# Expert weights of a routed layer in twelve transfers per expert instead of six

## The reference

```python
for e in range(N_EXPERTS):
    hh = xf @ w_expert_in[e] + b_expert_in[e]            # (264, 2048)
    gate = min(hh[:, :1024], 7); lin = clip(hh[:, 1024:], -7, 7)
    act = (lin + 1) * gate * sigmoid(1.702 * gate)
    y += comb[:, e:e+1] * (act @ w_expert_out[e] + b_expert_out[e])
```

## Time and profile before

| | us |
|---|---|
| median of 3 runs | 1761.41 (1759.38 to 1762.2) |
| profiled execution, own time | 1761.88 |
| its span, first to last instruction | 1760.1 |
| TensorE busy with products | 1566.7 (89% of the span) |
| VectorE / ScalarE / GpSimd busy | 306.7 / 208.8 / 143.8 |
| read from HBM / written | 507.62 MB / 30.50 MB |
| chain that ended last | 65% TensorE, 28% DMA, 3% VectorE |
| granted TensorE clock, mean | 0.939 of full speed |

### The profile page before, as it was taken

One profiled execution on the slowest core, in us unless ns is written; L12 is line 12 of the kernel. 1 busy time (PEld: TensorE's weight loads), 2 busy tenths in 40 slices (PEclk: granted clock), 3 DMA queues, 4 the chain that ended last, 5 costly groups with the idle time before them and its releaser, 6 DMA issues.

```text
span 1760.1 us, 18050 instructions
## 1 busy us (share of the span) xinstructions
PE 1566.7 (89%) x6938; PEld 755.9 (43%) x6939; DVE 306.7 (17%) x597; ACT 208.8 (12%) x369; POOL 143.8 (8%) x202
## 2 busy tenths in 40 slices
PE   5899999799949688999998999989898999999894
PEld 2687887651138465433333333333333333333331
DVE  1000000424341013211211111111111111111113
ACT  2100000424320001101000000000000000000001
POOL 0040000000107000000000000000000000000000
PEclk9899999889989889899999999999999999999997
DMA  8565656317950345555899999999999999999992
GB/s 316 188 224 188 238 191 229 108 48 282 336 196 28 143 161 221 202 206 235 339 424 418 422 424 418 420 420 422 418 427 419 412 413 414 409 421 419 426 417 81
DMA packets 78729, 533.55 MB, mean 303 GB/s; under 512 B 7290, under 2 KB 8402, under 8 KB 51842
## 3 DMA queue, kind: packets, MB, share of 16 engines
q1 hardware_dynamic: 66896, 502.35, 70.2%
q0 software_dynamic: 9952, 24.61, 4.6%
q10 hardware_dynamic: 1849, 6.16, 1.0%
HBM read 507.62 MB, written 30.50 MB: 306 GB/s over the span
## 4 chain that ended last, share of the span: by engine, by line
PE 65%; DMA 28%; DVE 3%; ACT 2%; SPq 1%; issue 1%; ACTq 0%; DVEq 0%; POOL 0%; POOLq 0%
DMA ring<-in_w_expert_in_dram 23%; PE ps L517 15%; PE ps L790 14%; PE ps L811 14%; PE ps L673 3%; PE ps L445 3%; PE ps L602 2%; PE ps L671 2%; PE ps L707 2%; PE ps L754 1%; PE ps L590 1%; PE ps L762 1%; DMA ring<-in_w_up_ret_dram 1%; PE ps L495 1%; PE ps L581 1%
## 5 line engine op out<-in xcount | busy, mean ns | idle before, releaser
L790 PE MATMUL ps<-ring,xgT 128*64 128x512 f32 x1632 | 409.9, 648 | 40.9 <-DMA ring<-in_w_expert_in_dram 40.9
L517 PE MATMUL ps<-hT,ring 128*128 128x264 f32 x1152 | 261.3, 389 | 4.7 <-ACT hT L896 4.7
L790 PEld LDWEIGHTS ps<-ring,xgT 128*64 128x64 f32 x1632 | 121.7, 148 | 305.5 <-issue 251.2
L811 PE MATMUL ps<-moe_ring,actT 128*64 128x512 f32 x1088 | 242.7, 599 | 0.4 <-ACT actT L1007 0.4
L517 PEld LDWEIGHTS ps<-hT,ring 128*128 128x128 f32 x1152 | 219.9, 192 | 49.5 <-issue 6.7
L811 PEld LDWEIGHTS ps<-moe_ring,actT 128*64 128x64 f32 x1088 | 78.1, 137 | 140.4 <-issue 135.5
L1293 DVE COPY xg<-ps 128x512 f32<-128x512 f32 x35 | 24.2, 691 | 622.8 <-PE ps L754 622.8
L790 PE MATMUL ps<-moe_ring,xgT 128*64 128x512 f32 x544 | 122.5, 592 | 0.0
L754 PE MATMUL ps<-rows,picked 128*64 128x512 f32 (+1 forms) x420 | 101.4, 599 | 1.6 <-ACT x_rows L991 1.6
L1003 ACT ACTIVATE glu_s<-glu_g 128x512 f32<-128x512 f32 x34 | 21.4, 629 | 448.8 <-DVE glu_g L1305 448.8
L790 PEld LDWEIGHTS ps<-moe_ring,xgT 128*64 128x64 f32 x544 | 39.1, 137 | 77.7 <-issue 77.7
(11 more groups left out here) (254 smaller groups left out, 986.3 us busy)
## 6 DMA issues: line engine op xcount, KB each, us to landing
ring<-in_w_expert_in_dram SPq DMA_DIRECT2D x96, 2048.0 KB, 16.5
moe_ring<-in_w_expert_out_dram SPq DMA_DIRECT2D x64, 2048.0 KB, 10.7
moe_ring<-in_w_expert_in_dram SPq DMA_DIRECT2D x32, 2048.0 KB, 18.1
ring<-in_w_in_dram SPq DMA_DIRECT2D x18, 2048.0 KB, 8.0
ring<-in_w_ada_dram SPq DMA_DIRECT2D x12, 2048.0 KB, 11.4
ring<-in_state_ret_dram SPq DMA_DIRECT2D x8, 2048.0 KB, 11.5
out_dram<-ring POOLq DMA_DIRECT2D x8, 2048.0 KB, 11.5
ring<-in_w_up_ret_dram SPq DMA_DIRECT2D x4, 2048.0 KB, 13.9
```

Source lines behind the costliest of these rows:

```text
L517: mm = nc.tensor.matmul(ps[:, j, 0:T], ring[s][:, k, j * P:(j + 1) * P], hT[:, k, :], start=(k == 0), stop=(k == KC - 1))
L790: mm = nc.tensor.matmul(side(bank, g), xgT[:, 2 * j + a, :], w[:, a, c * COL:(c + 1) * COL], start=False, stop=(j == 3 and a == 1))
L811: mm = nc.tensor.matmul(side(2, g), actT[:, 4 * h + a, :], w[:, a, g * COL:(g + 1) * COL], start=False, stop=(h == 1 and a == 3))
```

## The change

- Each of the six chunks becomes two of 1 MB, 8 KB in each partition, in half of the old place: eight (j = 0 to 7) for `w_expert_in`, of 128 rows each, one row in a partition; four (8 to 11) for `w_expert_out`, of 256 rows each, two in a partition. SP issues twelve transfers for an expert, and each is waited for by itself.
- The places in memory stay as they were; two new chunks lie where an old one lay. TensorE's order is the same: what stood after old chunk 0 now stands after new chunks 0 and 1, and so on. The number and size of its products are the same.
- The uses of all eight input chunks count on one semaphore (`in_used`), those of the four output chunks on another (`out_used`), instead of one for each chunk. Both are raised at the start by one item's worth. Every wait on them is rewritten to a count. Most come at the same instruction as before; those of GpSimd on the first chunk of either kind come after the first half of the old chunk.
- The transposes read contiguous columns for the input chunks, and every second for the output chunks.
- Three semaphores that nothing used are gone (`c_sig`, `rstd_ready`, `osq_free`), and so are the six of `chunk_used`.

```diff
-CHUNKS = 6
+SLOTS_IN, SLOTS_OUT = 8, 4
+CHUNKS = SLOTS_IN + SLOTS_OUT
...
-        moe_ring = list(ring) + [new(f"moe_ring{s}", [P, KC, COL]) for s in range(RING, CHUNKS)]
+        for s in range(3):
+            new(f"moe_space{s}", [P, KC, COL])
+        half_at = [ring_at + size([P, KC, COL]) * s for s in range(RING)] + [work + size([P, KC, COL]) * s for s in range(3)]
+        moe_ring = [at(f"moe_ring{j}", [P, 2 * D], half_at[j // 2] + size([P, 2 * D]) * (j % 2)) for j in range(CHUNKS)]
...
             def expert(e, j):
-                if j < 4:
-                    src = w_expert_in[0, e, 2 * P * j:2 * P * (j + 1)].rearrange("(p a) n -> p (a n)", a=2)
+                if j < SLOTS_IN:
+                    src = w_expert_in[0, e, P * j:P * (j + 1)]
                 else:
-                    src = w_expert_out[0, e, COL * (j - 4):COL * (j - 3)].rearrange("(p a) n -> p (a n)", a=4)
-                sp.dma_start(moe_ring[j][:].rearrange("p k n -> p (k n)"), src).then_inc(moe_loaded[j], 16)
+                    src = w_expert_out[0, e, 2 * P * (j - SLOTS_IN):2 * P * (j - SLOTS_IN + 1)].rearrange("(p a) n -> p (a n)", a=2)
+                sp.dma_start(moe_ring[j][:], src).then_inc(moe_loaded[j], 16)
...
-                for j in range(CHUNKS):
-                    sp.wait_ge(chunk_used[j], due)
+                for j in range(SLOTS_IN):
+                    sp.wait_ge(in_used, due * SLOTS_IN + (j + 1))
                     expert(e, j)
+                for h in range(SLOTS_OUT):
+                    sp.wait_ge(out_used, due * SLOTS_OUT + (h + 1))
+                    expert(e, SLOTS_IN + h)
...
+            pe.sem_inc(in_used, SLOTS_IN)
+            pe.sem_inc(out_used, SLOTS_OUT)
...
             def hidden(j, e):
                 pe.wait_ge(moe_loaded[j], e * 16 + 16)
-                w = moe_ring[j][:].rearrange("p k n -> p (k n)").rearrange("p (a n) -> p a n", a=2)
-                for a in range(2):
-                    for bank in range(2):
-                        for g in range(2):
-                            c = 2 * bank + g
-                            mm = nc.tensor.matmul(side(bank, g), xgT[:, 2 * j + a, :], w[:, a, c * COL:(c + 1) * COL],
-                                                  start=False, stop=(j == 3 and a == 1))
-                mm.then_inc(chunk_used[j], 1)
+                for bank in range(2):
+                    for g in range(2):
+                        c = 2 * bank + g
+                        mm = nc.tensor.matmul(side(bank, g), xgT[:, j, :], moe_ring[j][:, c * COL:(c + 1) * COL],
+                                              start=False, stop=(j == SLOTS_IN - 1))
+                mm.then_inc(in_used, 1)
...
-                for h in range(2):
-                    pe.wait_ge(moe_loaded[4 + h], e * 16 + 16)
-                    w = moe_ring[4 + h][:].rearrange("p k n -> p (k n)").rearrange("p (a n) -> p a n", a=4)
-                    for a in range(4):
+                for h in range(SLOTS_OUT):
+                    j = SLOTS_IN + h
+                    pe.wait_ge(moe_loaded[j], e * 16 + 16)
+                    for a in range(2):
                         for g in range(2):
...
-                    mm.then_inc(chunk_used[4 + h], 1)
+                    mm.then_inc(out_used, 1)
...
-                act_e.wait_ge(chunk_used[3], q + 1)
+                act_e.wait_ge(in_used, q * SLOTS_IN + 2 * SLOTS_IN)
...
-                pool.wait_ge(chunk_used[0], q + 1)
+                pool.wait_ge(in_used, q * SLOTS_IN + (SLOTS_IN + 1))
```

More of the change, by code:

```diff
@@ L320, in trunk_kernel @@
         moe_loaded = [sem(f"moe_loaded{s}") for s in range(CHUNKS)]
-        chunk_used = [sem(f"chunk_used{s}") for s in range(CHUNKS)]
+        in_used, out_used = sem("in_used"), sem("out_used")
         picked_ready, slots_ready, slots_taken = sem("picked_ready"), sem("slots_ready"), sem("slots_taken")
@@ L419, in _ @@
                 due = sp.value_load(cum_i[0:1, e - 1:e], min_val=1, max_val=ITEMS)
-                for j in range(CHUNKS):
-                    sp.wait_ge(chunk_used[j], due)
+                for j in range(SLOTS_IN):
+                    sp.wait_ge(in_used, due * SLOTS_IN + (j + 1))
                     expert(e, j)
+                for h in range(SLOTS_OUT):
+                    sp.wait_ge(out_used, due * SLOTS_OUT + (h + 1))
+                    expert(e, SLOTS_IN + h)
             items = sp.value_load(cum_i[0:1, E - 1:E], min_val=E, max_val=ITEMS)
-            for j in range(2):
-                sp.wait_ge(chunk_used[j], items)
+            for j in range(1):
+                sp.wait_ge(in_used, items * SLOTS_IN + SLOTS_IN)
                 sp.sem_inc(sp_pace, 1)
@@ L766, in turn_gathered @@
                 pe.wait_ge(xg_taken, q + 1)
-                for c in range(2):
-                    for a in range(2):
-                        mm = turn(ps[:, 3, (2 * c + a) * P:(2 * c + a + 1) * P], xg[:, 2 * P * c:2 * P * (c + 1)].rearrange("s (p a) -> s a p", a=2)[:, a, :])
+                for c in range(4):
+                    mm = turn(ps[:, 3, c * P:(c + 1) * P], xg[:, c * P:(c + 1) * P])
                 mm.then_inc(xg_turned, 1)
@@ L805, in outward @@
                 pe.wait_ge(act_taken, q + 1)
[L806 to L809 removed]
+                for h in range(SLOTS_OUT):
+                    j = SLOTS_IN + h
+                    pe.wait_ge(moe_loaded[j], e * 16 + 16)
+                    for a in range(2):
                         for g in range(2):
[L811 to L813 removed]
+                            mm = nc.tensor.matmul(side(2, g), actT[:, 2 * h + a, :], moe_ring[j][:, a * D + g * COL:a * D + (g + 1) * COL],
+                                                  start=False, stop=(h == SLOTS_OUT - 1 and a == 1))
+                    mm.then_inc(out_used, 1)
             gather(0)
@@ L821, in _ @@
             hidden(0, 0)
+            hidden(1, 0)
             pe.wait_ge(slots_taken, SLOT_STEPS)
             pick(1, second)
-            hidden(1, 0)
-            gather(1)
             hidden(2, 0)
             hidden(3, 0)
+            gather(1)
+            hidden(4, 0)
+            hidden(5, 0)
+            hidden(6, 0)
+            hidden(7, 0)
             turn_gathered(1)
@@ L835, in _ @@
                 hidden(0, e)
+                hidden(1, e)
                 turn_hidden(q - 1)
@@ L839, in _ @@
                 outward(q - 1, before)
-                hidden(1, e)
-                gather(q + 1)
                 hidden(2, e)
                 hidden(3, e)
+                gather(q + 1)
+                hidden(4, e)
+                hidden(5, e)
+                hidden(6, e)
+                hidden(7, e)
                 turn_gathered(q + 1)
@@ L1016, in _ @@
             squash(0)
[L1017 removed]
+            act_e.wait_ge(in_used, 2 * SLOTS_IN)
             take_gathered(1)
@@ L1315, in _ @@
                 take_slots(q + 1, bass.ds(q + 1, 1))
-            for j in range(2, CHUNKS):
-                dve.wait_ge(chunk_used[j], items)
+            dve.wait_ge(in_used, items * SLOTS_IN + SLOTS_IN)
+            dve.wait_ge(out_used, items * SLOTS_OUT + SLOTS_OUT)
             step(nc.vector.memset(small[:, 2:5], 0.0))
```

26 lines of the change are left out of this document (12 added, 14 removed).

## The result

The kernel with the change takes 1766.68 us (median; 1765.02 to 1770.51) against 1761.41 before, a ratio of 1.0034 [1.0023, 1.0044]: 5.3 us slower, where 3.7 us faster was forecast. Its profiled execution took 1765.65 us with a span of 1763.9 us, 3.8 us more than the one of before on both counts.

A forecast was written before the change was run, and what follows sets the result against it. Bound: TensorE's pace until about 860 us, then the weight stream at 430 GB/s. Rows +7.5, entry -1.7, recovery -8.5, end -1.0 sum to -3.7 us: from the profiled 1761.88 to 1758.2 us; range 1749 to 1769.

The forecast's parts named there:

- The stream: Expert weight transfers after about 860 us: dearer 8 KB rows, +7.5 us, against recovered dry time, -8.5 us.
- Entry: Fourth expert's first output request: its first half is free after a quarter of the outward products, -1.7 us (bounds -1.8 and 0).
- rows of 8 KB: Expert weight stream: smaller packets cost 6.7 us, completions 0.8; together +7.5 us, bounds +3.8 and +31.
- The bound of 31 us: Expert weight stream: upper bound on the cost of 8 KB rows; at 414 GB/s they would cost 31.2 us.
- rival 2: Expert weight stream: small rows slower than assumed, deciding from 424 GB/s downwards; at 414, +18 us, 1779.9 us; chance 0.12.
- engines no longer dry: Later expert periods: requests 1.8 us earlier keep DMA engines from running dry, -8.5 us of 10.5 left over.
- signs of failure announced: Expert stream: clean rate under 424 GB/s, dips remaining despite earlier requests, or SP's requests longer than 0.33 us.
- Rival 1: Stretches behind output requests: dips are the memory's own, not starvation; +4.8 us, 1766.7 us; chance 0.18.
- End: Last expert: TensorE finishes its first chunk 1.8 us after the second half lands, not 3.65; -1.0 us taken.
- Requests and completions: SP's queue: twelve requests for six cost nothing (bounds 0 and 1 us); twice as many completions cost 0.8 us.

The follow-up runs named there:

- e6: The changed kernel run once more, unchanged; 1768.05 us, ratio 1.0037 to the kernel before.
- e3: The changed kernel, but both halves of an old chunk are requested only when both are free and awaited together; 1772.81 us, ratio 1.0066.
- e9: The kernel before, with the next item's first input chunk asked for on ScalarE's queue, three loads more; 1751.19 us, ratio 0.994.
- e1: The kernel before with rows of 8 KB, still six transfers of 2 MB an expert; 1771.56 us, ratio 1.0057.
- e8: The kernel before with only the first input chunk split into two transfers with 8 KB rows; 1757.87 us, ratio 0.998.
- e2: The kernel before with each chunk as two transfers of 64 partitions, rows of 16 KB, waited for together; median 2586.04 us.
- e12: The kernel before without the scatter of the expert results, whose part is missing from the output; 1732.08 us, ratio 0.9834.

## Why the prediction was wrong

Its mechanisms were at work, a dearer row against engines that run dry, but both sizes of the stream's sum were too favourable. In the prediction's own steps, against before (858.79, 836.5 and 64.8 us):

| step | forecast | after | e6 |
|---|---|---|---|
| first output request of the fourth expert | -1.7 | -3.0 | -1.7 |
| from it to the last expert's first 2 MB, on all engines | +7.5 - 8.5 = -1.0 | +8.2 | +8.1 |
| from there to the end | -1.0 | -1.4 | -2.4 |
| sum (spans) | -3.7 | +3.8 | +4.0 |

- **The stream is the step that failed: -1.0 us forecast, +8.2 measured.** Entry and end came out as forecast or better.
- **In it, rows of 8 KB: +7.5 us predicted, +11.6 measured.** The price came from the earlier trace rows: 428 GB/s gave 3.8 us, the packets' 7.3 ns a pair gave 9.6, and the middle, 6.7, was taken with the 9.6 called an upper reading; it was the better one. The text put the clean stretches at 426 to 428 GB/s. That is right for the first 10 us behind each scatter in the changed kernel, and wrong for the 64% of the clean stream that runs at the slow rhythm's 421.9. The bound of 31 us held the truth, and rival 2 named the point from which it decides: 424 GB/s. The measured level is 423.8. The profile of before had a hint, not followed up: clean cuts of 16 KB rows at 429 and at 431 in the earlier trace rows, two levels of one stream.
- **In it, engines no longer dry: -8.5 predicted, -5.5 measured in the mean of the engines and -3.4 where it counts** (8.2 less 11.6, at the last engine). The shortfall went from 9.8 to 4.3 us, not to under 3; dips remain (371 GB/s at 1526 us). The step took the mean rate for the time: a dip is time lost by the engines that are ahead, and a chunk waits for the last. Of the 3.4 us the earlier requests bring 0.3 (e3 against after); where the other 3.1, which e3 has too, come from stays open. Dips together with earlier requests was one of the signs of failure announced. Rival 1, dips that are the memory's own, gives 1766.7, next to the time measured, and is wrong all the same: e3 and e9 bring or remove dips by moving requests, with the rows as they were. It had the sum by luck, a row price 4.1 us too low against a recovery of nothing.
- **Entry: -1.7 predicted, -3.0 measured in after, -1.7 in e6.** The 857.0 forecast is e6's 857.10. After's profiled execution had the first item's 16 products on a chunk in 3.59 us, where they took 5.21 before: the clock stayed up there, which has nothing to do with halves and isn't so in e6.
- **End: -1.0 predicted, -1.4 and -2.4 measured** from the second half's landing (1700.53 and 1701.71). From TensorE's start on the second half 62.8 and 62.3 us are left, 62.6 were forecast. Counted from its start on the first half, it is 65.8 us in after and 64.8 in e6 against 64.4, since a longer wait leaves the clock low behind it (5.35 us for 16 products in after), as the text had said.
- **Requests and completions: 0.8 us taken for completions, 0 for the rest; e1 against after shows none** (clean 424.1 and 423.8). SP's four output requests follow one another at 1.7 us (four in 5.48), TensorE's pace for half a chunk; a request itself takes the 0.33 us of before.

From the forecast of 1758.2 to the median of 1766.68 are 8.5 us: 4.1 by the rows' price and 5.1 by the recovery, less 0.7 that entry, end and the choice of the execution leave. Had only the rows' price been right, the forecast would have been 1762.3, no change.

## What to carry to other kernels

A saturated stream's price per packet has to be read where the stream runs for long, not in its first 10 us: 1.5% of rate was 11.6 us here. What a dip in the mean rate costs has to be read at the engine that lands last: here the mean said 2.4 us for the earlier requests, and the last engine 0.3. Before transfers are cut smaller to get their requests out sooner, look for a second queue on an engine with time to spare: the earlier request is then had with the large rows (e9, -10.7 us, most of it at the end), and where one must split, split the one chunk on which something waits (e8, -3.5 us).

## What the runs showed of the hardware

- Transfers of 64 partitions, one behind the other on one queue, ran at half the rate for most of the stream: 218 GB/s in 1000 to 1400 us, 1253 ns for a 16 KB packet where transfers of 128 partitions have 611, with all 16 engines busy (e2). The Trainium skill (DMA: Bandwidth & Descriptors, "Rules for kernel authors") says of two transfers to disjoint partition halves not to bother; here the kernel took 1.40 times as long with them.
- A stream of equal packets has two rhythms (8 KB: 309 ns or 311 to 319; 16 KB: 611 or 612 to 625). In the slow one a packet costs 9.6 ns beyond its bytes, in the fast one some 5; rows of 8 KB fall into the slow one some 10 us behind a scatter on another queue. The Trainium skill (the same page, "Why small descriptors are slow") gives about 3 cycles a packet, an estimate of 3.5 ns at the fabric's clock that it gives; the runs show more.
- The 16 engines don't keep step: a 1 MB transfer's shares landed 5.5 us apart (after), and 0.7 us apart for 2 MB without a scatter (e12).
- Twice as many queued transfers of half the size cost nothing that shows (e1 against after, 424.1 and 423.8 GB/s). The Trainium skill (the same page, "Anatomy of one DMA") counts about 2 us for each transfer, in a fit for GpSimd's path; on SP's queue nothing of the kind shows once transfers queue.
